# Odd-layer attention: the negated maxima spread once per query group and carried by 64 rows of the low score product

## The reference, cut to what matters

```python
q, k, v = jnp.split(h @ w_in, ...)
s_loc = jnp.where(allowed, einsum('bhgnqd,bhnkd->bhgnqk', qb, kb) * scale, NEG)
s_ctx = einsum('bhgnqd,bhkd->bhgnqk', qb, ck) * scale
p = softmax(concatenate([s_ctx, s_loc, s_sink], -1))[..., without the sink]
o = einsum(p_ctx, cv) + einsum(p_loc, vb)
return o @ w_out
```

## Time and profile before

| | us |
|---|---|
| median of 3 runs | 2759.65 |
| lowest and highest run | 2758.34, 2760.72 |
| span of the profiled execution, first to last instruction | 2755.2 |
| PE busy (share of the span) | 2631.6 (96%) |
| DVE busy | 1495.7 (54%) |
| ACT busy | 1044.2 (38%) |
| POOL busy | 3.7 (0%) |

### The profile page before, as it was taken

How to read it: one execution, slowest core, us unless ns; L and a number is a source line. 1 busy time by engine, 2 the same in 40 slices (tenths; PEclk the granted TensorE clock), 3 DMA queues, 4 the chain that set the end, 5 groups by cost and what they waited for, 6 DMA issues and landing times.

```text
span 2755.2 us, 41342 instructions
## 1 busy us (share of the span) xinstructions
PE 2631.6 (96%) x16891; PEld 2493.4 (90%) x16915; DVE 1495.7 (54%) x2411; ACT 1044.2 (38%) x1590; POOL 3.7 (0%) x5
## 2 busy tenths in 40 slices
PE   6999999999987999999999999999989989999998
PEld 6999999896557899999998999998978879999998
DVE  6888434634556477743467774346555446322334
ACT  4333334444553452223455222345333255222332
POOL 0000000000000000000000000000000000000000
PEclk7999999999999999999999999999989999999999
DMA  6666234321000165523446552343310024322344
GB/s 242 211 201 207 83 126 148 131 77 32 1 24 16 54 208 183 190 88 116 148 138 212 180 181 85 124 148 123 95 40 1 1 62 130 100 76 71 111 149 136
DMA packets 87770, 320.17 MB, mean 116 GB/s; under 512 B 12487, under 2 KB 16599, under 8 KB 87127
## 3 DMA queue, kind: packets, MB, share of 16 engines
q1 hardware_dynamic: 87638, 318.37, 35.7%
HBM read 312.44 MB, written 3.23 MB: 115 GB/s over the span
## 4 chain that ended last, share of the span: by engine, by line
PE 85%; DVE 7%; ACT 3%; issue 2%; DMA 1%; SPq 1%; another core or an unknown queue 0%; DVEq 0%; ACTq 0%
PE ps L2189 43%; PE ps L2218 29%; PE ps L999 2%; PE ps L755 2%; DVE w_lo L417 1%; PE ps L608 1%; ACT w_hi L411 1%; DMA w_raw<-in_ffn_gu 1%; PE ps L2252 1%; PE ps L985 1%; DVE hx_lo L1986 1%; DVE xsq L1977 1%; PE ps L556 1%; PE ps L988 1%; PE ps L987 1%
## 5 line engine op out<-in xcount | busy, mean ns | idle before, releaser
L417 DVE TENSOR_TENSOR w_lo<-w_raw,w_hi 128x1024 fp32r<-128x1024 f32 (+1 forms) x384 | 521.1, 1358 | 902.6 <-ACT w_hi L411 901.5
L411 ACT CAST w_hi<-w_raw 128x1024 fp32r<-128x1024 f32 (+1 forms) x384 | 444.0, 1157 | 1208.6 <-PE ps L2189 714.1
L2189 PE MATMUL ps<-hx_hi,w_hi 128*128 128x320 f32 x2688 | 613.7, 309 | 11.7 <-DVE hx_lo L1536 5.7
L2189 PE MATMUL ps<-hx_hi,w_lo 128*128 128x320 f32 x2688 | 612.5, 308 | 0.0
L2189 PE MATMUL ps<-hx_lo,w_hi 128*128 128x320 f32 x2688 | 612.2, 308 | 0.0
L2189 PEld LDWEIGHTS ps<-hx_hi,w_hi 128*128 128x128 f32 x2688 | 451.0, 188 | 13.0 <-issue 7.5
L2189 PEld LDWEIGHTS ps<-hx_lo,w_hi 128*128 128x128 f32 x2688 | 450.8, 188 | 0.0
L2189 PEld LDWEIGHTS ps<-hx_hi,w_lo 128*128 128x128 f32 x2688 | 450.8, 188 | 0.0
L2218 PE MATMUL ps<-hh_hi,w_hi 128*128 128x320 f32 x1408 | 435.1, 309 | 3.0 <-DVE hh_lo L2081 3.0
L2218 PE MATMUL ps<-hh_hi,w_lo 128*128 128x320 f32 x1408 | 433.0, 308 | 0.0
L2218 PE MATMUL ps<-hh_lo,w_hi 128*128 128x320 f32 x1408 | 433.0, 308 | 0.0
(11 more groups left out here) (300 smaller groups left out, 2626.0 us busy)
## 6 DMA issues: line engine op xcount, KB each, us to landing
w_raw<-in_ffn_gu SPq DMA_DIRECT2D x212, 512.0 KB, 3.6
w_raw<-in_ffn_dn SPq DMA_DIRECT2D x128, 704.0 KB, 4.1
ring_a<-in_ada_w SPq DMA_DIRECT2D x96, 512.0 KB, 4.5
ada_top<-in_ada_w SPq DMA_DIRECT2D x32, 512.0 KB, 4.6
w_raw<-in_even_in SPq DMA_DIRECT2D x16, 512.0 KB, 3.6
w_raw<-in_odd_in SPq DMA_DIRECT2D x12, 512.0 KB, 4.5
first_a<-in_ada_w SPq DMA_DIRECT2D x8, 512.0 KB, 11.9
w_raw<-in_even_out SPq DMA_DIRECT2D x8, 512.0 KB, 3.6
```

What stands on the lines that cost most here:

```text
L411: nc.scalar.copy(w_hi[:, slot, 0:tiles * P], w_raw[:, slot, 0:tiles * P]).then_inc(hi_done, 1)
L417: nc.vector.tensor_tensor(w_lo[:, slot, 0:tiles * P], w_raw[:, slot, 0:tiles * P], w_hi[:, slot, 0:tiles * P], ALU.subtract).then_inc(lo_d ...
L2189: last = nc.tensor.matmul(ps[:, out_bank + h, 0:TH], w, a[:, k, h * TH:(h + 1) * TH], start=(start and w is wh and a is hi), stop=(stop an ...
```

## The change

The negated maxima are no longer spread by a product in each block. Once per group PE makes the product ones x `diag_o` into bank 0 ("shift", a new kind of step; it waits for `fresh_max` and until all units issued so far have been read), and ACT scales rows 64 to 127 of it by 1/64 into rows 64 to 127 of a new buffer, `q_shift[:, group % 2]`. Into its rows 0 to 63 ACT copies the high halves of the group's four query heads, two copies of 64x256 (`act_shift_query`), at the group's third unit; they wait until all blocks of the group before the previous one have their scores, as the two share a buffer. Rows 64 to 127 of `k_lo` are filled with 1.0 by GpSimd, once, so the low product `k_lo` x `q_shift` gives the low keys by the high queries plus the negated maximum. The product of the two low halves is left out. DVE makes `k_lo` in 64 rows only, so `k_ready` counts three instead of four.

The plan is changed too. The context's four units stand behind the first block of tile 0's step instead of at the end of the step before (or, for the first head, in the projection); the units of the next tile stand two behind each of the following two blocks; the shift of a group stands behind the fourth block of the step before (behind the fifth in tile 0's step, behind the third for the context). In the first block of a group, the values of the block before stand ahead of the scores. A unit that uses bank 0 waits until every shift issued has been scaled (`w_shifted`), and so do the first scores of a group.

```diff
 def swa_plan():
-    units = [[("unit", g, i) for g in step for i in range(4)] for step in steps] + [[]]
...
+    def units(g, *which):
+        return [("unit", g, i) for i in which]
     for t, step in enumerate(steps):
         own = [(g, j) for g in step for j in range(len(g["blocks"]))]
-        per = -(-len(units[t + 1]) // (len(own) - 2))
+        ahead, first = [[] for _ in own], 0
+        if len(step) > 1:
+            ahead[0], first = units(step[1], 0, 1, 2, 3), 1
+        if t + 1 < len(steps):
+            g = steps[t + 1][0]
+            ahead[first] = units(g, 0, 1)
+            ahead[first + 1] = [("shift", x, 0) for x in step[1:]] + units(g, 2, 3)
+            ahead[first + 3] += [("shift", g, 0)]
...
+    start = steps[0][0]
+    plan, before, turning, low = units(start, 0, 1, 2, 3) + [("shift", start, 0)], None, [], []
...
+        now = [("scores",) + block] if block else []
         if before:
-            plan.append(("values",) + before)
+            value = [("values",) + before]
+            now = value + now if block and block[1] == 0 else now + value
...
-    return plan, start
+    return plan, 4
...
-                pe.wait_ge(k_ready, 4)
+                pe.wait_ge(k_ready, 3)
...
+            units, shifts = 4, 0
             for kind, g, x in SWA_PLAN[SWA_FIRST:]:
                 if kind == "unit":
+                    units += 1
+                    if units % 2:
+                        pe.wait_ge(w_shifted, shifts)
                     pe_unit(pe, g, x)
+                elif kind == "shift":
+                    pe.wait_ge(fresh_max, g["g"] + 1)
+                    pe.wait_ge(unit_read, units)
+                    shifts += 1
+                    nc.tensor.matmul(ps[:, 0, :], ones_r[:], diag_o[:, g["g"] % 4].rearrange("p i q -> p (i q)"),
+                                     start=True, stop=True).then_inc(w_spread, 1)
...
                     if x == 0:
-                        pe.wait_ge(fresh_max, g["g"] + 1)
+                        pe.wait_ge(w_shifted, g["g"] + 1)
...
-                    nc.tensor.matmul(out, ones_r[:], diag_o[:, g["g"] % 4].rearrange("p i q -> p (i q)"),
-                                     start=True, stop=False)
-                    nc.tensor.matmul(by_head, k_hi[:, h, kcol:kcol + P], queries, start=False, stop=False)
-                    ins = nc.tensor.matmul(by_head, k_lo[:, h, kcol:kcol + P], queries, start=False, stop=side is None)
+                    nc.tensor.matmul(by_head, k_hi[:, h, kcol:kcol + P], queries, start=True, stop=False)
+                    ins = nc.tensor.matmul(out, k_lo[:, h, kcol:kcol + P], q_shift[:, g["g"] % 2], start=False,
+                                           stop=side is None)
...
+        def act_shift_query(act, g):
+            h = g["h"]
+            act.wait_ge(q_hi_done, 2 * h + 2)
+            if g["g"] >= 2:
+                act.wait_ge(w_st_ready, SWA_GROUPS[g["g"] - 1]["b"])
+            copy = q_shift[0:64, g["g"] % 2].rearrange("p (i q) -> p i q", q=P)
+            for e in range(2):
+                nc.scalar.copy(copy[:, e:4:2], q_two[64 * e:64 * e + 64, 4 * h + e:4 * h + 4:2,
+                                                     g["q0"]:g["q0"] + P].bitcast(F32))
...
         def act_swa(act):
+            act_shift_query(act, SWA_GROUPS[0])
             for kind, g, x in SWA_PLAN[SWA_FIRST:]:
-                if kind == "scores":
+                if kind == "unit" and x == 2:
+                    act_shift_query(act, g)
+                elif kind == "shift":
+                    act.wait_ge(w_spread, g["g"] + 1)
+                    nc.scalar.mul(q_shift[64:P, g["g"] % 2], ps[64:P, 0, :], 1 / 64).then_inc(w_shifted, 1)
+                elif kind == "scores":
...
-            nc.vector.tensor_tensor(k_lo[:, :, T:], k_old[:], k_hi[:, :, T:].bitcast(F32), ALU.subtract)
+            nc.vector.tensor_tensor(k_lo[0:64, :, T:], k_old[0:64], k_hi[0:64, :, T:].bitcast(F32), ALU.subtract)
...
-                for half in range(2):
-                    nc.vector.tensor_tensor(k_lo[64 * half:64 * half + 64, e:KV_HEADS:2, 0:T], qk_raw[rows, 0:2, :],
-                                            k_hi[rows, e:KV_HEADS:2, 0:T].bitcast(F32), ALU.subtract).then_inc(k_ready, 1)
+                nc.vector.tensor_tensor(k_lo[0:64, e:KV_HEADS:2, 0:T], qk_raw[rows, 0:2, :],
+                                        k_hi[rows, e:KV_HEADS:2, 0:T].bitcast(F32), ALU.subtract).then_inc(k_ready, 1)
...
+                elif s["kind"] == "mix":
+                    pool.wait_ge(mix_loaded, 16 * (7 + 3))
+                    nc.gpsimd.memset(k_lo[64:P, :, :].bitcast(F32), 1.0).then_inc(k_ready, 1)
```

More of the change, by code:

```diff
@@ L127, in swa_plan @@
     steps = swa_groups()
-    units = [[("unit", g, i) for g in step for i in range(4)] for step in steps] + [[]]
     rows, late = [], {0: {1: ("turn", 8), 3: ("turn", 9)}, 1: {0: ("halve", 8), 2: ("halve", 9)}}
+    def units(g, *which):
+        return [("unit", g, i) for i in which]
     for t, step in enumerate(steps):
         own = [(g, j) for g in step for j in range(len(g["blocks"]))]
-        per = -(-len(units[t + 1]) // (len(own) - 2))
+        ahead, first = [[] for _ in own], 0
[6 more added lines that the diff above has]
+            ahead[first + 3] += [("shift", g, 0)]
         for i, block in enumerate(own):
-            rows.append((block, units[t + 1][(i - 1) * per:i * per] if i else [], late.get(t, {}).get(i)))
-    plan, before, turning, low = list(units[0]), None, [], []
-    start = len(plan)
+            rows.append((block, ahead[i], late.get(t, {}).get(i)))
+    start = steps[0][0]
+    plan, before, turning, low = units(start, 0, 1, 2, 3) + [("shift", start, 0)], None, [], []
     for block, ahead, extra in rows + [(None, [], None)] * 3:
@@ L139, in swa_plan @@
         low = []
-        if block:
-            plan.append(("scores",) + block)
         ending = []
+        now = [("scores",) + block] if block else []
         if before:
-            plan.append(("values",) + before)
+            value = [("values",) + before]
+            now = value + now if block and block[1] == 0 else now + value
             if before[1] == len(before[0]["blocks"]) - 1:
                 ending = [before[0]]
-        plan += ahead
+        plan += now + ahead
         if extra:
@@ L224, in build @@
                 esb(name, [P, KT, T])
+            with ExitStack() as part:
+                q_shift = part.enter_context(nc.sbuf_tensor("q_shift", [P, 2, 512], F32R))
             esb("below_tmp", [P, 2, T])
@@ L343, in build @@
         w_sink_arg, w_sink_exp = sem("w_sink_arg"), sem("w_sink_exp")
+        w_spread, w_shifted = sem("w_spread"), sem("w_shifted")
         w_st_ready, w_p_ready, w_pv_done = sem("w_st_ready"), sem("w_p_ready"), sem("w_pv_done")
@@ L1027, in evacuate @@
                 if n in (4, 5):
-                    act.wait_ge(k_ready, 4)
+                    act.wait_ge(k_ready, 3)
                     act.wait_ge(out_stored, 16 * 6)
```

## The result

The kernel before takes 2757.96 us (median of 20 runs), the changed one 2762.47 (20 runs, 2758.13 to 2774.31); the ratio is 1.0022, 95% interval [1.0015, 1.0030]. The forecast was 3.2 us faster. The sign is the other one: the interval leaves out no change, though the 4.5 us are fewer than the 5.5 that the prediction took as the least that a measurement tells. The time lies within the range given.

What follows compares the result with a forecast made beforehand. TensorE was taken to bound the kernel nearly everywhere. Start -1.4, products -13.1, context's first units +0.4 and waits +10.9 sum to -3.2 us: span 2752.0, time 2756.4 us; range 2747 to 2767 us.

Steps and rivals of the forecast that it cites:

- The price of a product: Attention blocks: each spread product removed from TensorE saves 0.23 us, not the 0.48 us of its row.
- (a): Each head, before tile 1's third unit: TensorE waits until ACT has scaled the context's spread product in bank 0; 0.85 us.
- (b): Each head, before the values of tile 0's last block: query copies stand ahead of its exponential on ACT; 0.8 us.
- (c): Each head, before the context block's value products, now ahead of tile 1's first scores: a wait of 0.6 us.
- (d): Each head, before tile 1's first value products: two reductions on DVE delay the low half they need; 1.25 us.
- (e): Each head, context's four units behind tile 0's first scores: DVE's divisors and reductions delay the third; about 0.8 us.
- (d) of the first head: Head 1, before tile 1's first value products: DVE's rounding for late queries lengthens the wait to 2.9 us.
- The start: Projection to first scores: context units leave (-2.75 us), query copies and first scaling on ACT come in (+1.4); -1.4 us.
- The stretch at half clock behind that wait I let stand: Head 1, behind the 1.84 us wait of before: clock 0.54 from 2037.94 to 2041.69, taken as unchanged.
- the clock rival: Attention: added waits lower TensorE's clock, 1.57 us a fall; once a head 2762.7 us (0.08), twice 2769.0 us (0.14).
- the row against it: From 836 to 850 TensorE was idle 3.4 of 14 us at full clock; cited against the clock rival.
- The covered-waits rival: Each head: (a) to (c) vanish if scaling and copies are faster and ACT runs ahead; -12.2 us, 2747.4 us, chance 0.24.

Runs made afterwards that it cites:

- the start alone filled: Changed kernel, tile 1's query copies behind the exponential of tile 0's last block, unread products at the start alone (8 and 3): 2752.06 us, ratio 0.9976.
- the fastest version: Changed kernel, tile 1's query copies behind the exponential of tile 0's last block, 21 unread products (start, first head's (d)): 2746.09 us, ratio 0.9963.
- the filled kernel: Changed kernel with unread products at the start and at (a), (b), (c) and (d): 2754.10 us, ratio 0.9986.
- the control: Kernel before with unread products at the start (8) and ahead of the first head's 1.84 us wait (7): 2753.96 us, ratio 0.9985.

## Why the prediction was wrong, point by point

**The price of a product** held: 0.23 us forecast, 17.2 / 76 = 0.23 measured.

**The waits** held, one by one (from issue to issue, shown wait plus 0.16): (a) 0.85 forecast, 0.84 measured; (b) 0.8 and 0.89; (c) 0.6 and 0.61; (d) 1.25 and 1.07; (e) 0.8 and 0.63. Sum 4.4 and 4.04 us. The scaling took 0.59 us against 0.60 taken; the two copies 0.82 against 0.74. A middle head at full clock was to take 41.4 us and takes 41.55. (d) of the first head was to be 2.9 us; the 2.72 shown with the start alone filled is 2.88.

**The start** held: first scores 1.5 us earlier against the first unit (20.73 to 19.24 us), 1.4 forecast. GpSimd's fill is one of 64x3584, not the 64x5120 that I read; it took 3.09 us and nobody waited for it.

**By heads, at full clock.** Where a head of the changed kernel fell, I take its length from a kernel in which it didn't: the first from the fastest version with (b) added again (42.46 + 0.89), the fourth from the filled one. For before, the first head comes from the control. These are estimates. The first head of the filled kernel agrees with 43.35: 44.94 us with one stretch of 3.4 us, which costs some 1.6 in the kernel before (46.43 to 44.89, to 43.21). The forecast is laid out by the same stretches here: one of the first head's 15 products stands ahead of its first low product, and 0.81 us of value products move from the last head's stretch to the first one's.

| | forecast | at full clock |
|---|---|---|
| start, to the first scores | -1.4 | -1.5 |
| first scores to first low product | one product, -0.23 | 0.34 - 0.57 = -0.23 |
| head 1 | 14 products, -3.22, +1.8 of waits, +0.81: -0.6 | 43.35 - 43.21 = +0.15 |
| heads 2 and 3 | -0.57 each | -0.42 each |
| head 4 | -3.22 + 3.8 + 0.4 - 0.81 = +0.2 | 41.20 - 40.18 = +1.0 |
| sum | -3.2 | -1.4 |

Two terms were off, those of the first and the last head, by 0.8 us each. In the last head one wait is not in the sum: where no next units stand, the values of the last group's first block wait for their exponential, 0.22 us as shown, 0.38 from issue to issue. I did not take the rest apart.

```profile
2199.76 1.10 PE L1020 MATMUL ps<-v_aug,prob_o 128*128 128x65 f32 x8 [0.22 <-ACT prob_o L1119]
```

The sign would still have been right, and the gain too small to measure.

**The step that failed is "The stretch at half clock behind that wait I let stand"**: the sum put the change of the clock at nothing, and the chances of the clock rival, 0.08 and 0.14, were too low with it. In the profiled pair the time at half clock grew from 6.8 to 47.8 us. The first head lost 54.70 - 43.35 = 11.35 us to it after, and 0.25 more lie ahead of its first low product; before, it lost 46.43 - 43.21 = 3.2. The second head lost 2.3, the fourth 2.4. Together 11.6 - 3.2 + 2.3 + 2.4 = 13.1, and with the -1.4 of the table that makes 11.7, the growth of the stage. This has to come out, since the lengths at full clock stand in both terms; what it rests on is those lengths, which come from other runs. For the medians I have no trace, only the mean granted clock of each run, 0.976 in the middle after and 0.979 before: 0.003 of 2760 us is 16.6 us more at half clock; at the 13.1 us that 41 more of them cost here, some 5 us, with -1.4 about +4 against the +4.5 measured (an estimate, since the clock is given to three decimals). The runs with unread products say the same without it: filling gave back 8.4 us after and 4.0 before.

Three things were wrong within that rival. I priced a fall at 1.57 us from one stretch of 3.4 us; such a one costs that (46.43 - 44.89 = 1.54 at the start), but those of the second and fourth heads lasted 6.83 us and cost 2.3 each. I counted falls by waits, one or two in each head, when what came was one long stretch at the start, where 1.4 us of new ACT work stood directly behind a wait that was already there, and two falls at (b) and (c). And I used the row against it, 3.4 idle of 14 us at full clock, as if idle time in one stage spoke for idle time in another. My own rule, that the clock decides the sign from about three falls on, was met. That the rival's time for one fall a head, 2762.7 us, lies next to the 2762.47 measured is luck: neither the number of the falls nor their length was the one it counted with.

The Trainium skill's page TensorE: Matmul & The Clock Gate warns in its Part 1, under "A second HAM failure mode: psum-queue depth-cycling", that frequent short idle times between groups of products can make the clock swing. The falls behind waits of 0.73 and 0.45 us agree with that; the third head, with the same waits and no fall, shows that they need not come.

**The rest.** I took 4.45 us around the span; it is 1.8 to 2.0, so the forecast in its own terms should have read about 2754. The covered-waits rival (0.24) got no support: none of (a) to (e) vanished.

## What to carry to other kernels

When a change takes work off the bounding engine and puts short waits in its place, price the clock with the waits: look in the profile of before for the places where the granted clock already falls, and ask first whether the change adds idle time just ahead of or behind one. That isn't enough by itself: the falls of the second and fourth heads came where the profile of before had none. Where waits are added, look for an order that takes the wait away (here one ScalarE step moved behind an exponential); where none was at hand, a handful of products that nobody reads held the clock here. And give the kernel before the same help when you judge the change, or the help is counted as the change's.

## What the runs showed of the hardware that I had not expected

TensorE's clock can stay at half for long with the engine at work: 34.13 us in the first head, with PE busy for 30.01 of them, and 10.24 us with PE busy in all of them where the start was filled and the copies moved. Eleven unread products in front of the first scores removed that stretch, and in the profile with fillers at the waits inside the head alone it was 10.2 us; what ends such a stretch stays open. Equal waits did not always bring a fall: the second and fourth heads fell, the third, with the same waits, did not, and the times of one and the same kernel spread with it (2758.13 us at a mean clock of 0.979, 2774.31 at 0.972). And filling a wait leaves the waits as long as they were (41.48 us against 41.55 for a head at full clock): what the unread products give back is clock alone.
